# Half rows for the expert outputs of a mixture-of-experts decoder step

## The chip, the cores and the metric

The kernel runs on one core of one Trainium2 chip. The metric is the device time of one execution in microseconds (us), lower is better. Every matrix is float32.

## The reference

The reference computes one layer of a hybrid decoder for 512 prompt tokens and 8 sample tokens, D = 1024: an RMS norm, one combined projection, differential attention and indexed sparse attention in parallel, gates, an output projection and a residual. After it comes the hierarchical mixture of experts, which is all that the change touches:

```python
h = rmsnorm(x, g_ffn).reshape(b * t, d)
...
top_val, top_idx = lax.top_k(e_in_group, 2)          # inside the best of 4 groups
top_w = jax.nn.softmax(top_val, axis=-1) * g_w
...
for each of the 32 experts (wg, wu: 1024x512, wd: 512x1024):
    act = silu(h @ wg) * (h @ wu)
    out = out + (act @ wd) * combine_weight[:, None]
y = x + out
```

Each of the 520 tokens goes to two experts, so the 32 experts have 1040 token rows together, 32.5 on average. The weights of an expert are three matrices of 2 MB.

## The kernel before, in words

The kernel has four stages, each a block in which every engine has its own instruction stream: projection, attention of the prompt, merge (L1107 to L1773), and experts (L1776 on). An engine leaves a block only when all have come to its end. This document is about the last steps of merge and about the expert stage.

**Tables.** Merge routes the tokens and builds, with products of one-hot matrices on TensorE (L1342, L1347, L1351), for each expert a list of up to CAP = 64 tokens in order of rank. The list is written twice in PSUM, for partitions 0 to 63 and for 64 to 127, since the rows of tokens are handled as halves: partition p below 64 has the first 512 columns of the p-th token, partition 64 + p has the other 512. VectorE turns the list into integer tables (L1765 to L1770): `s.halves` (128 partitions) is the row number in the array of half rows, 2 x token + half, and a number beyond every bound (from NO_ROW) where the expert has no token. `s.table` (64 partitions) is the row in the prompt's output, `s.to_s` (64 partitions) the row in the sample's output, each with a number out of bounds where the row isn't there. `share(3)` and L1773 follow; the latter puts the weight of each token and expert on 128 partitions. Then merge ends.

**The loop over experts.** For expert e = 0 to 31, with two sets of buffers:
- GpSimd gathers the half rows of the expert after the next (`gather_rows`, L157): one indirect DMA, 128 rows of 2 KB from DRAM to 128 partitions; rows out of bounds are skipped.
- TensorE transposes them (L1821), VectorE copies them with the gain of the norm (L1977), TensorE multiplies by the gate and the up weights (L1827), ScalarE and VectorE make the activation (L1951, L2044, L2049), TensorE transposes it (L1833) and multiplies by the down weights (`down_product`, L1841). The result Y lies in one PSUM bank as 128 partitions of 512 columns: output columns 0 to 511 of token slot p at partition p, columns 512 to 1023 at partition 64 + p.
- ScalarE scales Y by the weights and writes y, a tile of 64 partitions of 1024 columns, in two operations (L1956), one for each half: the second reads partitions 64 to 127 and writes partitions 0 to 63. It waits for the adds of expert e - 2, which read the same buffer.
- GpSimd adds y to the outputs in DRAM (`add_rows`, L2084 to L2090): an indirect DMA with an addition to the prompt's output y_p (L2085) and one to the sample's output y_s (L2088), each over all 64 rows of 4 KB; those out of bounds write nothing.

The order on GpSimd's queue is, in pass e: wait until expert e's rows are transposed; gather for expert e + 2; wait for y of expert e - 1; wait until the adds of expert e - 2 have landed (`y_added`); issue the two adds of expert e - 1. So the adds of two experts never run beside each other, and a gather comes behind the adds that were issued before it.

**Weights.** SyncE issues the loads of the weights (L1103) in an order written out by hand, as soon as one of 4, 4 and 3 places for gate, up and down is free (`g_done`, `u_done`, `d_done`). They run in queue q1. GpSimd's DMAs run in queue q0.

**Extra blocks.** Experts with over 64 tokens get further blocks in a loop over a count that is known at run time (`extra`, `step`). VectorE prepares their tables as it does the first (L2032 to L2038). The profile of this data shows none of them carried out, but it has the tables made at the end. The last thing that SyncE waits for is `y_added`.

Of the kernel before, what the change touches and what calls it, by code (L numbers as in the profile page):

```python
# [7 lines left out]
F32, I32 = mybir.dt.float32, mybir.dt.int32  # L8
ALU = mybir.AluOpType
# [1106 lines left out]
def merge(nc, io, s):  # L1116
# [3 lines left out]
    with ExitStack() as ctx:  # L1120
# [32 lines left out]
        Lm, Lm2, C = (small[:, 40 + 32 * n:72 + 32 * n] for n in range(3))  # L1153
        unfilled, early, twice = small[:, 232:232 + NE], small[0:CAP, 264:264 + NE], small[:, 392:392 + NE]
        prank = small[:, 296:296 + 2 * NE].rearrange("p (k e) -> p k e", k=2)
# [370 lines left out]
        def _(dve):  # L1526
# [240 lines left out]
            v.tensor_tensor(s.halves[:, 0:NE], twice, unfilled, ALU.add).then_inc(table_ready, 1)  # L1767
            v.scalar_tensor_tensor(s.table[:, 0:NE], TBt[0:CAP, :], -1.0, unfilled[0:CAP, :], ALU.add, ALU.add)
            link(v.tensor_scalar(early, TBt[0:CAP, :], 1.0 + SEQ, NO_ROW, ALU.is_lt, ALU.mult))
            link(v.scalar_tensor_tensor(s.to_s[:, 0:NE], TBt[0:CAP, :], -1.0 - SEQ, early, ALU.add, ALU.add))  # L1770
            share(3)
# [4 lines left out]
def experts(nc, io, s):  # L1776


    with ExitStack() as ctx:
        sb = lambda n, sh, dt=F32: ctx.enter_context(nc.sbuf_tensor("e_" + n, sh, dt))  # L1780
        ps = lambda n, sh: ctx.enter_context(nc.psum_tensor("e_" + n, sh, F32))
        sem = lambda n: ctx.enter_context(nc.semaphore("e_" + n))
        idx = sb("idx", [128, 3], I32)
        xg = s.xg
# [4 lines left out]
        aT = sb("aT", [128, 2, 128])  # L1789
        y = [sb(f"y{n}", [CAP, D]) for n in range(2)]  # L1790
        TX, AT = ps("TX", [128, 4, 2 * CAP]), s.bankO[:, 0:256].rearrange("p (f t) -> p f t", f=2)
# [5 lines left out]
        eid = spare[:, 180:180 + NX + 1]  # L1797
        unfilled, early, twice = spare[:, 200:200 + NX], spare[0:CAP, 216:216 + NX], spare[:, 232:232 + NX]
        cmp = spare[:, 256:256 + NE * NX].rearrange("p (a b) -> p a b", a=NE)
# [144 lines left out]
        @block.scalar  # L1944
        def _(act):
            for e in range(NE):
                j = e % 2
                act.wait_ge(g_done, e + 1)
                if e:
                    act.wait_ge(a_ready, e)  # L1950
                nc.scalar.activation(sig[:], G[j][:, 0:HW], ACT.Sigmoid).then_inc(gated, 1)  # L1951
                act.wait_ge(d_done, e + 1)
                if e >= 2:
                    act.wait_ge(y_added, 32 * (e - 1))
                for h in range(2):
                    last = nc.scalar.activation(y[j][:, W * h:W * h + W], Y[j][CAP * h:CAP * h + CAP, :], ACT.Copy,  # L1956
                                                scale=s.share[CAP * h:CAP * h + CAP, e:e + 1])
                last.then_inc(y_out, 1)

            def step(act, b):  # L1960
                act.wait_ge(g_done, b + NE + 1)
                nc.scalar.activation(sig[:], G[0][:, 0:HW], ACT.Sigmoid).then_inc(gated, 1)
                act.wait_ge(d_done, b + NE + 1)
                act.wait_ge(y_added, b * 32 + NE * 32)
                for h in range(2):
                    last = nc.scalar.activation(y[0][:, W * h:W * h + W], Y[0][CAP * h:CAP * h + CAP, :], ACT.Copy,
                                                scale=s.share[CAP * h:CAP * h + CAP, bass.ds(b + NE, 1)])
                last.then_inc(y_out, 1)
                act.nop()
            extra(act, step)  # L1970

        @block.vector
        def _(dve):
# [55 lines left out]
            def tables_out():  # L2029

                dve.wait_ge(extra_tabled, 1)
                link(v.tensor_scalar(unfilled, TB[:, 0:NX], 0.0, NO_ROW, ALU.is_equal, ALU.mult))  # L2032
                link(v.tensor_scalar(twice, TB[:, 0:NX], 2.0, s.c[:, C_HALF:C_HALF + 1], ALU.mult, ALU.add))
                link(v.tensor_tensor(s.halves[:, NE:NBLK], twice, unfilled, ALU.add))
                link(v.scalar_tensor_tensor(s.table[:, NE:NBLK], TB[0:CAP, 0:NX], -1.0, unfilled[0:CAP, :], ALU.add, ALU.add))
                link(v.tensor_scalar(early, TB[0:CAP, 0:NX], 1.0 + SEQ, NO_ROW, ALU.is_lt, ALU.mult))
                link(v.scalar_tensor_tensor(s.to_s[:, NE:NBLK], TB[0:CAP, 0:NX], -1.0 - SEQ, early, ALU.add, ALU.add))
                v.tensor_copy(s.share[:, NE:NBLK], TB[:, NX:2 * NX]).then_inc(extra_ready, 1)  # L2038
# [39 lines left out]
        def _(pool):  # L2078
# [5 lines left out]
            def add_rows(n, rows, to_s):  # L2084
                nc.gpsimd.indirect_dma_start(out=io["y_p"], out_offset=bass.IndirectOffsetOnAxis(ap=rows, axis=0),  # L2085
                                             in_=y[n][:], in_offset=None, bounds_check=SEQ - 1, oob_is_err=False,
                                             compute_op=ALU.add).then_inc(y_added, 16)
                nc.gpsimd.indirect_dma_start(out=io["y_s"], out_offset=bass.IndirectOffsetOnAxis(ap=to_s, axis=0),  # L2088
                                             in_=y[n][:], in_offset=None, bounds_check=NS - 1, oob_is_err=False,
                                             compute_op=ALU.add).then_inc(y_added, 16)  # L2090

            for e in range(NE + 1):
                if e + 2 < NE:
                    pool.wait_ge(x_turned, e + 1)
                    gather_rows(nc, s, e % 2, s.halves[:, e + 2:e + 3])
                if e == NE:
                    n_extra = extra_blocks(pool)
                if e:
                    pool.wait_ge(y_out, e)
                if e >= 2:  # L2100
                    pool.wait_ge(y_added, 32 * (e - 1))
                if e:
                    add_rows((e - 1) % 2, s.table[:, e - 1:e], s.to_s[:, e - 1:e])

            def step(pool, b):
                pool.wait_ge(y_added, b * 32 + NE * 32)
                pool.wait_ge(x_turned, b + NE)
                nc.gpsimd.tensor_copy(idx[:, 0:1], s.halves[:, bass.ds(b + NE, 1)]).then_inc(idx_ready, 1)
                nc.gpsimd.tensor_copy(idx[0:CAP, 1:2], s.table[:, bass.ds(b + NE, 1)]).then_inc(idx_ready, 1)
                nc.gpsimd.tensor_copy(idx[0:CAP, 2:3], s.to_s[:, bass.ds(b + NE, 1)]).then_inc(idx_ready, 1)  # L2110
                pool.wait_ge(idx_ready, b * 4 + 3)
                pool.sem_inc(idx_ready, 1)
                gather_rows(nc, s, 0, idx[:, 0:1])
                pool.wait_ge(y_out, b + NE + 1)
                pool.sem_inc(y_passed, 1)
                add_rows(0, idx[0:CAP, 1:2], idx[0:CAP, 2:3])
                pool.wait_ge(y_added, b * 32 + NE * 32 + 32)
# [8 lines left out]
def step_kernel(nc, io):  # L2126
# [14 lines left out]
    with ExitStack() as top:  # L2141
# [48 lines left out]
        s.gffn = sb("gffn", [128, KD])  # L2190
        s.table, s.ctl = sb("table", [CAP, NBLK], I32), sb("ctl", [1, NX + 1], I32)
        s.halves = sb("halves", [128, NBLK], I32)
        s.to_s = sb("to_s", [CAP, NBLK], I32)
        s.share = sb("share", [128, NBLK])
# [41 lines left out]
```

## Time and profile before

| | us |
|---|---|
| median of 3 runs (1139.65 to 1141.88) | 1140.24 |
| the profiled execution | 1139.45 |
| its span, from the first instruction to the end | 1137.6 |
| TensorE matmul busy | 1015.8 (89%) |
| VectorE busy | 433.5 (38%) |
| GpSimd busy | 302.4 (27%) |
| ScalarE busy | 243.2 (21%) |

The mean granted TensorE clock is 0.981. The span of the profiled execution is 1.85 us shorter than its own time, which lies 0.79 us under the median. In the profile, PE is TensorE, DVE VectorE, ACT ScalarE, POOL GpSimd and SP SyncE; a name like e_y is a tile of the expert stage, x_ and k_ are tiles that live longer, and g_ those of merge. A row "A <-B 5.0" says that the engine sat idle for 5.0 us before it and that B ended that. Row counts of DMA queues are packets; the share is the time that they took, of 16 DMA engines over the window.

### The profile page before, as it was taken

Reading aid. Unit: us, or ns where it says so; the run is one execution under the profiler, and the core shown is the slowest. Engines: PE = TensorE matmul, PEld = TensorE weight load, DVE = VectorE, ACT = ScalarE, POOL = GpSimd, SP = SyncE. Lnnn points to the kernel's source line nnn. Section 1 sums busy time; section 2 is a strip of 40 time slices with the busy share of each in tenths; the row PEclk is TensorE's granted clock in tenths of the full one; section 3 lists DMA queues with packets and bytes.
Section 4 is the critical chain, followed back from the end, with each engine's and each line's share of the span. In section 5 each row is a group of like instructions: output and inputs, shape, how many; then the busy total and the mean of one; then the engine's idle time right before and its main releaser. Section 6 shows DMA issues by size and latency. Waiting matters only on the chain. (4 is left out here: it accounts for less than half of the span.)

```text
span 1137.6 us, 15848 instructions
## 1 busy us (share of the span) xinstructions
PE 1015.8 (89%) x5861; PEld 563.7 (50%) x5861; DVE 433.5 (38%) x1202; ACT 243.2 (21%) x550; POOL 302.4 (27%) x262
## 2 busy tenths in 40 slices
PE   6999999998999999998999679999987877777776
PEld 3644444445777776332455444455444434444443
DVE  3545888886566574322324411111110111011122
ACT  2122221212444545301024201111111110111011
POOL 1023513532555444001000113233322212221222
PEclk9999999999999999999999789999999999999999
DMA  6330232217656444888392789999999999999993
GB/s 207 94 109 20 75 103 103 94 44 244 195 191 212 141 135 159 315 328 296 110 426 94 277 361 412 414 421 416 412 416 419 423 416 416 416 423 415 418 411 118
DMA packets 82465, 304.26 MB, mean 267 GB/s; under 512 B 23117, under 2 KB 27341, under 8 KB 70227
## 3 DMA queue, kind: packets, MB, share of 16 engines
q1 hardware_dynamic: 64658, 273.47, 61.4%
q0 software_dynamic: 9824, 16.98, 5.1%
q10 hardware_dynamic: 7904, 12.78, 3.1%
q8 instruction: 47, 0.77, 0.3%
q14 instruction: 32, 0.25, 0.1%
HBM read 290.09 MB, written 29.72 MB: 281 GB/s over the span
## 5 line engine op out<-in xcount | busy, mean ns | idle before, releaser
L404 PE MATMUL p_z<-k_w,k_xT 128*128 128x512 f32 (+2 forms) x528 | 208.9, 550 | 0.3 <-DMA k_w<-in_w_in 0.3
L404 PEld LDWEIGHTS p_z<-k_w,k_xT 128*128 128x128 f32 (+1 forms) x528 | 92.2, 188 | 103.2 <-issue 101.4
L872 PE MATMUL a_G<-k_xT,k_w 128*128 128x260 f32 x512 | 127.2, 393 | 0.0
L2044 DVE TENSOR_TENSOR e_hid<-e_hid,e_G 128x256 f32<-128x256 f32 x32 | 13.5, 421 | 259.1 <-ACT e_hid L1951 259.1
L1956 ACT ACTIVATE e_y<-e_Y,x_share 64x512 f32<-64x512 f32 x64 | 43.7, 683 | 303.9 <-PE e_Y L1841 286.5
L872 PEld LDWEIGHTS a_G<-k_xT,k_w 128*128 128x128 f32 x512 | 92.9, 191 | 26.6 <-issue 13.8
L967 POOL TENSOR_TENSOR k_x<-k_x 128x512 f32<-128x512 f32 x64 | 80.5, 1271 | 89.5 <-DVE k_side L1033 69.2
L2085 POOL DMA_INDIRECT out_y_p<-e_y,x_table x32 | 46.2, 1443 | 201.9 <-ACT e_y L1956 132.5
L157 POOL DMA_INDIRECT k_rows<-token_rows,x_halves x32 | 33.7, 1054 | 155.4 <-PE e_TX L1821 144.7
L1243 PE MATMUL g_ring<-k_oT,k_w 128*128 128x512 f32 x128 | 60.1, 616 | 0.0
L2049 DVE TENSOR_TENSOR e_hid<-e_hid,e_U 128x256 f32<-128x256 f32 x32 | 13.5, 421 | 116.9 <-PE e_U L1827 116.9
L942 ACT ACTIVATE a_prob<-a_masked,a_nb 128x128 f32<-128x128 f32 (+3 forms) x64 | 36.0, 562 | 70.2 <-DVE a_nb L1047 70.2
L2088 POOL DMA_INDIRECT out_y_s<-e_y,x_to_s x32 | 45.4, 1420 | 9.8 <-issue 9.8
L1841 PE MATMUL e_Y<-k_xT,e_aT 128*64 128x512 f32 x176 | 40.2, 598 | 8.5 <-DVE e_aT L2053 8.5
L1841 PE MATMUL e_Y<-x_page,e_aT 128*64 128x512 f32 x176 | 40.2, 598 | 7.2 <-DVE e_aT L2053 7.2
L1033 DVE TENSOR_REDUCE k_side<-k_x 128x8 f32<-128x512 f32 x64 | 43.1, 674 | 1.5 <-POOL k_x L967 1.4
L1841 PE MATMUL e_Y<-x_w_out,e_aT 128*64 128x512 f32 x160 | 36.5, 598 | 6.6 <-DVE e_aT L2053 6.6
L556 POOL TENSOR_TENSOR p_tb<-p_t,q_rg 128x512 f32<-128x512 f32 (+1 forms) x20 | 35.4, 1772 | 22.0 <-DVE p_t L614 22.0
L1827 PE MATMUL e_G<-x_w_out,e_xT 128*64 128x256 f32 x256 | 32.2, 404 | 8.2 <-DMA x_w_out<-in_w_gate 8.2
L548 POOL TENSOR_SCALAR p_rs<-p_ms 128x8 f32<-128x8 f32 (+1 forms) x20 | 3.9, 195 | 132.5 <-DVE p_ms L581 132.5
L1827 PE MATMUL e_G<-k_w,e_xT 128*64 128x256 f32 x256 | 32.3, 405 | 7.2 <-DMA k_w<-in_w_gate 6.4
L1243 PEld LDWEIGHTS g_ring<-k_oT,k_w 128*128 128x128 f32 x128 | 23.8, 194 | 29.5 <-issue 29.2
(357 smaller groups left out, 1476.1 us busy)
## 6 DMA issues: line engine op xcount, KB each, us to landing
k_w<-in_w_in SPq DMA_DIRECT2D x11, 2048.0 KB, 8.8
k_xT<-in_w_down SPq DMA_DIRECT2D x11, 2048.0 KB
x_page<-in_w_down SPq DMA_DIRECT2D x10, 2048.0 KB, 38.5
x_w_out<-in_w_down SPq DMA_DIRECT2D x10, 2048.0 KB
k_w<-in_w_gate SPq DMA_DIRECT2D x8, 2048.0 KB, 37.1
k_w<-in_w_up SPq DMA_DIRECT2D x8, 2048.0 KB
k_oT<-in_w_gate SPq DMA_DIRECT2D x8, 2048.0 KB
k_side<-in_w_up SPq DMA_DIRECT2D x8, 2048.0 KB
```

Of the source, the lines that this page charges most:

```text
L404: last = nc.tensor.matmul(z[u % 3][0:p, 0:WIDTH[k]], s.xT[:, j, 128 * i:128 * i + p], s.w[:, c % 2, j, 0:WIDTH[k]], start=j == 0, stop=j = ...
L556: nc.gpsimd.tensor_tensor(tb[0:p, :].rearrange("p (h d) -> p h d", h=H), t0[0:p, :].rearrange("p (h d) -> p h d", h=H), bcast(s.rg[0:p, g, ...
L872: last = nc.tensor.matmul(G[u % 2][:, 0:HT], s.w[:, q % 2, j, 128 * c:128 * c + 128], s.xT[:, j, HT * h:HT * h + HT], start=j == 0, stop=j ...
L942: nc.scalar.activation(prob[:, n % 4, 0:w], masked[:, n % 3, 0:w], ACT.Exp, bias=nb[:, n:n + 1], scale=DH ** -0.5, accum_out=sums[:, n:n + ...
L967: nc.gpsimd.tensor_tensor(prods[:, m % 2, :], page[:, m % KEY_PLACES, :], qB[:, nq % 2, :], ALU.mult).then_inc(k_used, 1)
L1033: nc.vector.tensor_reduce(s.sT[k][:, n, H * b:H * b + H], prods[:, m % 2, :].rearrange("p (h d) -> p h d", h=H), AX.X, ALU.add).then_inc(k ...
L1243: last = nc.tensor.matmul(bank[:], s.wo[k][:, j, first:first + 128], x[:, j, 0:SEQ], start=j == 0, stop=j == NB - 1)
L1827: last = nc.tensor.matmul(pair(bank[CAP * h:CAP * h + CAP, 0:HW]), xT[:, j, b, :], own(weight_row(s, n, r, b), h), start=b == 0, stop=b == ...
L1841: last = nc.tensor.matmul(bank[CAP * h:CAP * h + CAP, :], aT[:, b % 2, CAP * (b // 2):CAP * (b // 2) + CAP], weight_row(s, 2, r, b)[:, W * ...
L1956: last = nc.scalar.activation(y[j][:, W * h:W * h + W], Y[j][CAP * h:CAP * h + CAP, :], ACT.Copy, scale=s.share[CAP * h:CAP * h + CAP, e:e ...
L2085: nc.gpsimd.indirect_dma_start(out=io["y_p"], out_offset=bass.IndirectOffsetOnAxis(ap=rows, axis=0), in_=y[n][:], in_offset=None, bounds_c ...
L2088: nc.gpsimd.indirect_dma_start(out=io["y_s"], out_offset=bass.IndirectOffsetOnAxis(ap=to_s, axis=0), in_=y[n][:], in_offset=None, bounds_c ...
```

## The change

The output tiles y keep the shape that Y has in PSUM, 128 partitions of 512 columns. One ScalarE operation of 128 partitions takes the place of the two of 64. The adds go over 128 rows of 2 KB with the outputs seen as arrays of half rows, and take their row numbers for the prompt from `s.halves`, the table of the gather. `s.table` and the VectorE operation that made it are gone; `s.to_s` is made on 128 partitions from `twice`. The same is done to the tables and to the loop of the extra blocks, which has two copies of indices on GpSimd instead of three.

```diff
@@ merge
-            v.scalar_tensor_tensor(s.table[:, 0:NE], TBt[0:CAP, :], -1.0, unfilled[0:CAP, :], ALU.add, ALU.add)
-            link(v.tensor_scalar(early, TBt[0:CAP, :], 1.0 + SEQ, NO_ROW, ALU.is_lt, ALU.mult))
-            link(v.scalar_tensor_tensor(s.to_s[:, 0:NE], TBt[0:CAP, :], -1.0 - SEQ, early, ALU.add, ALU.add))
+            link(v.tensor_scalar(early, TBt, 1.0 + SEQ, NO_ROW, ALU.is_lt, ALU.mult))
+            link(v.scalar_tensor_tensor(s.to_s[:, 0:NE], twice, -2.0 * SEQ, early, ALU.add, ALU.add))
@@ experts
-        y = [sb(f"y{n}", [CAP, D]) for n in range(2)]
+        y = [sb(f"y{n}", [128, W]) for n in range(2)]
+        y_half = {n: io["y_" + n].rearrange("t (h d) -> (t h) d", h=2) for n in "ps"}
...
-                for h in range(2):
-                    last = nc.scalar.activation(y[j][:, W * h:W * h + W], Y[j][CAP * h:CAP * h + CAP, :], ACT.Copy,
-                                                scale=s.share[CAP * h:CAP * h + CAP, e:e + 1])
-                last.then_inc(y_out, 1)
+                nc.scalar.activation(y[j][:], Y[j][:], ACT.Copy, scale=s.share[:, e:e + 1]).then_inc(y_out, 1)
...
             def add_rows(n, rows, to_s):
-                nc.gpsimd.indirect_dma_start(out=io["y_p"], out_offset=bass.IndirectOffsetOnAxis(ap=rows, axis=0),
-                                             in_=y[n][:], in_offset=None, bounds_check=SEQ - 1, oob_is_err=False,
+                nc.gpsimd.indirect_dma_start(out=y_half["p"], out_offset=bass.IndirectOffsetOnAxis(ap=rows, axis=0),
+                                             in_=y[n][:], in_offset=None, bounds_check=2 * SEQ - 1, oob_is_err=False,
                                              compute_op=ALU.add).then_inc(y_added, 16)
...
-                    add_rows((e - 1) % 2, s.table[:, e - 1:e], s.to_s[:, e - 1:e])
+                    add_rows((e - 1) % 2, s.halves[:, e - 1:e], s.to_s[:, e - 1:e])
...
-                nc.gpsimd.tensor_copy(idx[0:CAP, 1:2], s.table[:, bass.ds(b + NE, 1)]).then_inc(idx_ready, 1)
-                nc.gpsimd.tensor_copy(idx[0:CAP, 2:3], s.to_s[:, bass.ds(b + NE, 1)]).then_inc(idx_ready, 1)
-                pool.wait_ge(idx_ready, b * 4 + 3)
+                nc.gpsimd.tensor_copy(idx[:, 1:2], s.to_s[:, bass.ds(b + NE, 1)]).then_inc(idx_ready, 1)
+                pool.wait_ge(idx_ready, b * 3 + 2)
...
-                add_rows(0, idx[0:CAP, 1:2], idx[0:CAP, 2:3])
+                add_rows(0, idx[:, 0:1], idx[:, 1:2])
```

The second add, to y_s, is changed as the first, and so are the ScalarE operation and the tables of the extra blocks.

## Rows read from the trace of the kernel before

**Rows 1.** The page, part 2: the span in forty slices.
```profile
PE   6999999998999999998999679999987877777776
...
DMA  6330232217656444888392789999999999999993
GB/s 207 94 109 20 75 103 103 94 44 244 195 191 212 141 135 159 315 328 296 110 426 94 277 361 412 414 421 416 412 416 419 423 416 416 416 423 415 418 411 118
```

**Rows 2.** Stretches of the expert stage: length, busy per engine, PEclk, DMA share, GB/s.
```profile
665.00:668.00 3.00, 3.00 (x28) 1.78 (x26) 0.26 (x1) 0.38 (x1) 0.00 (x0) 0.94 0.06 22
675.00:813.00 138.00, 132.31 (x950) 69.38 (x948) 20.52 (x44) 19.23 (x33) 43.16 (x33) 1.00 1.01 416
813.00:1116.00 303.00, 238.56 (x1647) 128.99 (x1645) 44.08 (x102) 34.59 (x59) 72.28 (x55) 0.99 1.01 416
```

**Rows 3.** The chain that ended last, in order of time, its end.
```profile
1076.52 43.32 DMA e_up<-in_w_up
...
1129.03 0.48 ACT e_y L1956
...
1129.73 0.69 ACT e_y L1956
...
1131.20 0.41 POOL out_y_p L2085
...
1132.92 1.42 POOL out_y_s L2088
```

**Rows 4.** DVE around the end of the merge stage, from the timeline.
```profile
647.55 0.18 DVE L1768 SCALAR_TENSOR_TENSOR x_table<-x_O,g_scp 64x32 int32<-64x32 f32 x1
647.65 0.17 DVE L1769 TENSOR_SCALAR g_scp<-x_O 64x32 f32<-64x32 f32 x1
...
650.33 0.19 DVE L1773 COPY x_share<-x_O 128x32 f32<-128x32 f32 x1 [1.13 <-PE x_O L1351]
...
650.90 0.61 PE L1895 MATMUL x_O<-x_Cpre,k_c 128*128 128x32 f32 x2 [0.68 <-PEq L1120]
```

**Rows 5.** Groups by line and shape, whole span: busy, mean ns, idle before and its releaser.
```profile
L2085 POOL DMA_INDIRECT out_y_p<-e_y,x_table x32 | 46.2, 1443 | 201.9 <-ACT e_y L1956 132.5 <-DMA out_y_s<-e_y,x_to_s 69.4
L2088 POOL DMA_INDIRECT out_y_s<-e_y,x_to_s x32 | 45.4, 1420 | 9.8 <-issue 9.8
L1956 ACT ACTIVATE e_y<-e_Y,x_share 64x512 f32<-64x512 f32 x64 | 43.7, 683 | 303.9 <-PE e_Y L1841 286.5 <-DMA out_y_s<-e_y,x_to_s 17.0
...
L157 POOL DMA_INDIRECT k_rows<-token_rows,x_halves x32 | 33.7, 1054 | 155.4 <-PE e_TX L1821 144.7 <-POOLq L1120 9.7 <-issue 1.0
...
L921 ACT ACTIVATE a_prob<-a_prob,a_inv 128x512 f32<-128x512 f32 x8 | 5.7, 711 | 0.0
```

**Rows 6.** DMA packets in 1128 to 1137.6 us, the last two adds alone.
```profile
DMA packets 161, 0.19 MB, mean 19 GB/s; under 512 B 117, under 2 KB 117, under 8 KB 160
...
q0 software_dynamic: 160, 0.18, 14.9%
```

**Rows 7.** DMA packets in 1001.7 to 1002.7 us, a gather's rows arriving.
```profile
q0 software_dynamic: 23, 0.09, 22.9%
```

**Rows 8.** DMA packets in 1008 to 1012 us, an add's rows leaving.
```profile
q0 software_dynamic: 92, 0.14, 17.7%
```

**Rows 9.** DMA packets in 868 to 872 us, only empty rows and counts on q0.
```profile
q1 hardware_dynamic: 120, 1.72, 100.5%
q0 software_dynamic: 52, 0.00, 0.7%
```

**Rows 10.** GpSimd's timeline, where TensorE sets the pace.
```profile
805.87 1.44 POOL L2085 DMA_INDIRECT out_y_p<-e_y,x_table  x1 [7.41 <-DMA out_y_s<-e_y,x_to_s]
...
818.61 1.44 POOL L2085 DMA_INDIRECT out_y_p<-e_y,x_table  x1 [7.63 <-DMA out_y_s<-e_y,x_to_s]
```

**Rows 11.** GpSimd's timeline, where the weights set the pace.
```profile
1003.64 1.44 POOL L2085 DMA_INDIRECT out_y_p<-e_y,x_table  x1 [5.00 <-ACT e_y L1956]
...
1019.87 1.44 POOL L2085 DMA_INDIRECT out_y_p<-e_y,x_table  x1 [5.34 <-ACT e_y L1956]
```

More of the change, by code:

```diff
@@ L1153, in merge @@
         Lm, Lm2, C = (small[:, 40 + 32 * n:72 + 32 * n] for n in range(3))
-        unfilled, early, twice = small[:, 232:232 + NE], small[0:CAP, 264:264 + NE], small[:, 392:392 + NE]
+        unfilled, early, twice = (small[:, n:n + NE] for n in (232, 264, 392))
         prank = small[:, 296:296 + 2 * NE].rearrange("p (k e) -> p k e", k=2)
@@ L1782, in experts @@
         sem = lambda n: ctx.enter_context(nc.semaphore("e_" + n))
-        idx = sb("idx", [128, 3], I32)
+        idx = sb("idx", [128, 2], I32)
         xg = s.xg
@@ L1797, in experts @@
         eid = spare[:, 180:180 + NX + 1]
-        unfilled, early, twice = spare[:, 200:200 + NX], spare[0:CAP, 216:216 + NX], spare[:, 232:232 + NX]
+        unfilled, early, twice = (spare[:, n:n + NX] for n in (200, 216, 232))
         cmp = spare[:, 256:256 + NE * NX].rearrange("p (a b) -> p a b", a=NE)
@@ L1964, in step @@
                 act.wait_ge(y_added, b * 32 + NE * 32)
[L1965 to L1968, printed above, removed]
+                nc.scalar.activation(y[0][:], Y[0][:], ACT.Copy, scale=s.share[:, bass.ds(b + NE, 1)]).then_inc(y_out, 1)
                 act.nop()
@@ L2034, in tables_out @@
                 link(v.tensor_tensor(s.halves[:, NE:NBLK], twice, unfilled, ALU.add))
-                link(v.scalar_tensor_tensor(s.table[:, NE:NBLK], TB[0:CAP, 0:NX], -1.0, unfilled[0:CAP, :], ALU.add, ALU.add))
-                link(v.tensor_scalar(early, TB[0:CAP, 0:NX], 1.0 + SEQ, NO_ROW, ALU.is_lt, ALU.mult))
-                link(v.scalar_tensor_tensor(s.to_s[:, NE:NBLK], TB[0:CAP, 0:NX], -1.0 - SEQ, early, ALU.add, ALU.add))
+                link(v.tensor_scalar(early, TB[:, 0:NX], 1.0 + SEQ, NO_ROW, ALU.is_lt, ALU.mult))
+                link(v.scalar_tensor_tensor(s.to_s[:, NE:NBLK], twice, -2.0 * SEQ, early, ALU.add, ALU.add))
                 v.tensor_copy(s.share[:, NE:NBLK], TB[:, NX:2 * NX]).then_inc(extra_ready, 1)
@@ L2084, in add_rows @@
             def add_rows(n, rows, to_s):
-                nc.gpsimd.indirect_dma_start(out=io["y_p"], out_offset=bass.IndirectOffsetOnAxis(ap=rows, axis=0),
-                                             in_=y[n][:], in_offset=None, bounds_check=SEQ - 1, oob_is_err=False,
+                nc.gpsimd.indirect_dma_start(out=y_half["p"], out_offset=bass.IndirectOffsetOnAxis(ap=rows, axis=0),
+                                             in_=y[n][:], in_offset=None, bounds_check=2 * SEQ - 1, oob_is_err=False,
                                              compute_op=ALU.add).then_inc(y_added, 16)
-                nc.gpsimd.indirect_dma_start(out=io["y_s"], out_offset=bass.IndirectOffsetOnAxis(ap=to_s, axis=0),
-                                             in_=y[n][:], in_offset=None, bounds_check=NS - 1, oob_is_err=False,
+                nc.gpsimd.indirect_dma_start(out=y_half["s"], out_offset=bass.IndirectOffsetOnAxis(ap=to_s, axis=0),
+                                             in_=y[n][:], in_offset=None, bounds_check=2 * NS - 1, oob_is_err=False,
                                              compute_op=ALU.add).then_inc(y_added, 16)
@@ L2190, in step_kernel @@
         s.gffn = sb("gffn", [128, KD])
-        s.table, s.ctl = sb("table", [CAP, NBLK], I32), sb("ctl", [1, NX + 1], I32)
+        s.ctl = sb("ctl", [1, NX + 1], I32)
         s.halves = sb("halves", [128, NBLK], I32)
-        s.to_s = sb("to_s", [CAP, NBLK], I32)
+        s.to_s = sb("to_s", [128, NBLK], I32)
         s.share = sb("share", [128, NBLK])
```

## The prediction

> **What bounds the kernel now.** First the forty slices: from the 24th on the DMA engines stand at 9 of 10 and move 411 to 426 GB/s in nearly every slice, while TensorE falls from 9 to 7 [rows 1]. So the stage to look at is the loop over experts, and its resource is the traffic of weights. The stretches say it more sharply [rows 2]: from 675 to 813 us both are full (TensorE 132.31 of 138 us, DMA share 1.01); from 813 to 1116 us TensorE is busy for 238.56 of 303 us and the DMA share is still 1.01. One stretch is empty: from 665 to 668 us the share is 0.06, because every place for weights was full and the first expert's product had yet to free one. From there on the end of the loop is a start plus bytes over rate.
>
> The chain that ended last confirms it: the last long wait is a load of up weights, 43.32 us up to 1119.85 us; then the last expert runs without cover, ScalarE from 1129.03 us, GpSimd's two adds from 1131.20 and 1132.92 us, and the landing of the second until the span ends at 1137.6 us [rows 3]. So three things can move the time: what comes before the loop's first product, the DMA engines' work per expert, and the tail behind the last load.
>
> **ScalarE.** Removed: two operations of 64x512, 683 ns each, 64 in all, 43.7 us of busy time [rows 5]. Added: one of 128x512 for each expert. No such form from PSUM with a scale for each partition is in the trace; the nearest is L921, 128x512 at 711 ns [rows 5], so the number of partitions costs next to nothing and I take 0.69 us, between 0.68 and 0.72. For 31 experts this gives nothing: TensorE waits for weights, and GpSimd's add waits for the landing of the earlier ones where TensorE sets the pace, 7.63 us before the one at 818.61 us [rows 10]. Under the last expert all of it counts: ScalarE now works from 1129.03 to 1129.73 + 0.69 = 1130.42 us, 1.39 us; it will be 0.69. **Minus 0.70 us.**
>
> **VectorE.** L1768 goes. It is not chained to the next one, so its cost is the step between the starts, 647.55 to 647.65 us, 0.10 us [rows 4]. Is it covered? VectorE is the last to leave merge: L1773 runs at 650.33 us for 0.19, and the first TensorE work of the next block comes at 650.90 us, 0.38 us later [rows 4]. The gathers, the first product, and so the restart of the loads after the empty stretch [rows 2] follow from it. **Minus 0.10 us.** The two operations that go from 64 to 128 partitions cost nothing: L1769 on 64 took 0.17 us and L1773 on 128 0.19 us [rows 4]. At the tail the table for extra blocks is off the path. The step loop isn't run.
>
> **GpSimd.** The adds are 64 instructions of 1443 and 1420 ns; the gather, with 128 indices and rows of 2 KB as the adds will have, is 1054 ns [rows 5]. So the new price isn't in the trace. Lower bound 1.05 us each: the addition costs nothing to describe and the half rows are as the gather's. Upper bound 2.88 us: the time goes by indices, and these double. I take 1.43, no change: the gather's 128 indices cost less than 64 of an add, so the index can't carry most of the cost. Two adds lie on the tail: between minus 0.76 and plus 2.9 us, taken as **0**.
>
> **The DMA engines.** Bytes stay: a valid row of 4 KB becomes two of 2 KB. What could change is packets and what each costs. The last two adds, alone in their window, have 160 packets on q0, 0.18 MB, and 117 under 512 B [rows 6]: 128 rows and 32 counts of the 16 engines. So a row of 4 KB is one packet now, and an empty row is a tiny one. Does a half row become a packet of its own? Of a gather, whose rows are 2 KB, one us shows 23 packets with 0.09 MB, about 4 KB for each [rows 7]: two half rows travel in one packet. I take the same for the adds: 64 packets for 128 half rows, as now. The time for each byte: 17.7% of 16 engines over 4 us, 11.3 us, for 0.14 MB, some 34 rows, is about 0.32 us for a row [rows 8], for the gather 22.9% of 16 us over 23 packets, 0.16 us [rows 7]: an add moves its bytes twice, and what is charged is bytes. **0**, if they pair. If they don't, 64 more tiny or split packets for each add come to 128 for each expert. A window of them alone shows 52 packets at 0.7% of 64 us, 9 ns each, with q1 at 100.5% [rows 9]: 128 x 9 ns / 16 is 0.07 us per expert, at most 2.2 us for 31. Their turns in the queue are another matter (second rival).
>
> The Trainium skill, DMA: Bandwidth & Descriptors, section "SWDGE vs HWDGE vs iDMA", says that a packet of such a queue is preferably up to 4096 B and is the boundary at which an engine switches queues. By that rule the count of packets stays; rows 7 agree. Its section "Why small descriptors are slow" speaks against the change: each operation carries 32 B of metadata besides a fixed cost per packet. If a row of 4 KB is one operation now, that is 128 more for each expert, 4 KB of traffic or an estimated 0.01 us at 416 GB/s, 0.3 us for the whole loop. No row shows it.
>
> **The sum.** 0.70 + 0.10 = 0.80 us less. Against the profiled execution: 1139.45 - 0.80 = 1138.65. That one lies 0.79 us under the median of the runs, so against the median 1140.24 - 0.80 = **1139.4 us**. A measurement of this kernel can tell about 0.2%, 2.3 us, from no change, so this counts as the same.
>
> **Rivals.** First, the add gets the gather's price on GpSimd: 0.37 us less for each, 0.76 us with both on the tail, so 1140.24 - 0.80 - 0.76 = 1138.7. For: same index count and row size. Against: the addition has to be described. It is still within 0.2%; more would need a shorter landing too. Chance 0.14.
>
> Second, slower by much: half rows of an add don't share packets. Its place is the wait for `y_added`, in which GpSimd holds the next adds. Where TensorE sets the pace, an add goes out at 805.87 and the next at 818.61 us, behind a wait of 7.63 us for the landing of the one before [rows 10]: a cycle of 12.74 us, of which issuing takes 1.44 + 0.30 + 1.42 = 3.16 us and landing 9.6. In it each engine has (64 + 16) x 2 / 16 = 10 packets of the adds, and waits its turn behind weights; with 144 for each add it has 18. At the same wait for each turn, landing takes 9.6 x 1.8 = 17.2 us, the cycle 20.4. But slower experts ask for fewer weights, so turns get shorter: the loop now passes 138 / 12.74 + 303 / 16.23 experts (16.23 from 1003.64 to 1019.87 us [rows 11]), some 29.5 in 441 us or 14.9 us for each, and with c for the cycle, c = 3.2 + 17.2 x 14.9 / c, so c = 17.7 us. The loop then takes 29.5 x 17.7 = 522 us: plus 81, about 1220. It decides from a cycle of 14.9 us, that is from about 12 packets for each engine. For: twice as many rows, and no row shows an addition with rows of 2 KB. Against: rows 7. The Trainium skill, same page, section "Queues, rings and completion order", has the engine take turns between queues by packets, which is this mechanism. Chance 0.12.
>
> Third, GpSimd's price goes by indices, 2.88 us each: plus 2.9 us on the tail and the cycle of 12.74 up to 15.6, over the 14.9 that the loop allows. With the cycle's part hidden 1142.3; with 0.7 us on 29.5 experts 1163. Against: the gather's 1.05 us. Chance 0.10.
>
> That the change doesn't do what it says is small: one operation on 128 partitions would have to take as long as two, which L921 excludes.
>
> **How the numbers follow.** The forecast has 0.64, its own range 1138.3 to 1140.9 (the bounds of ScalarE and an uncertain tail, and what runs differ by). Faster by over 0.2% (under 1138.0) takes an eighth of it and a part of the first rival: 0.10. Slower (over 1142.5): the second rival and two thirds of the third, 0.20. The rest, 0.70, is no change. The range goes from 1137.9, below the first rival, to 1142.8, the mild end of the third; outside it are the second rival and half of the third, and little on the fast side.
>
> **What would show it.** In the changed profile: L1956's successor 32 times at 0.68 to 0.72 us; the first add after ScalarE 0.7 us closer to the last down product; both adds at 1.43 us (first rival 1.05, third 2.88); 160 packets in the tail's window (288 by the second rival), and GpSimd's cycle at some 12.7 us where TensorE sets the pace; the DMA share at 1.01 over 675 to 1116 us; the first TensorE work of the expert block 0.1 us earlier. The prediction is wrong if the adds' cycle goes above 14.9 us, or if the weights' rate of 416 GB/s changes.

## The result, and the profile after

The changed kernel takes **1159.05 us** (median of 4 runs, 1156.46 to 1162.36) beside 1141.06 us for the kernel before on the same chip: a ratio of 1.0159, 95% interval 1.0128 to 1.0189. It is slower, and it lies outside the range 1137.9 to 1142.8. The profiled execution has 1158.48 us and a span of 1156.6 us, 19.0 us more than before.

The page of the changed kernel, the slices of part 2 and queue q0 of part 3 (packets, MB, share of 16 engines):

```profile
PE   6999999998999999989999499978787796878887
...
DMA  6231132226656446797482889999999999999971
GB/s 204 94 105 34 60 110 101 83 100 216 225 154 221 118 143 234 266 368 240 193 342 111 339 354 414 418 424 413 411 413 411 395 417 410 416 420 408 418 301 20
...
q0 software_dynamic: 13920, 17.00, 5.3%
```

and q0 on the page of before:

```profile
q0 software_dynamic: 9824, 16.98, 5.1%
```

The DMA rows look as in [rows 1]; q0 doesn't: 13920 packets for the same 17.0 MB instead of 9824. The difference is 4096, that is 32 experts x 2 adds x 64: **every add has 64 packets more**. The time of q0's packets hardly grows, from 5.1 to 5.3% of the 16 engines' span. TensorE is busy to the very end, also in the last slice, in which only 20 GB/s are moved. The stretches of the changed kernel (length, PE, PEld, DVE, ACT, POOL busy, PEclk, DMA share, GB/s):

```profile
675.00:813.00 138.00, 120.26 (x848) 62.55 (x844) 17.62 (x38) 10.15 (x20) 35.55 (x26) 0.95 1.02 417
813.00:1116.00 303.00, 245.49 (x1606) 123.93 (x1608) 38.33 (x84) 18.41 (x38) 78.90 (x57) 0.90 1.01 411
1116.00:1124.00 8.00, 7.48 (x52) 3.63 (x50) 3.98 (x12) 0.29 (x1) 3.63 (x3) 1.00 0.70 239
1124.00:1150.00 26.00, 24.39 (x175) 12.65 (x171) 5.92 (x16) 2.32 (x5) 9.35 (x6) 1.00 0.15 19
```

Against [rows 2]: in the first stretch TensorE is busy for 120.26 instead of 132.31 us, so it isn't the limit there any more, while the DMA share is still 1.02. The weights run nearly as before (411 instead of 416 GB/s from 813 to 1116 us) and are through shortly after 1124 us; from 1124 to 1150 us only 19 GB/s are moved, and TensorE works off what it lags behind. That lag is what the 19 us consist of. The groups by line and shape, from the page of the changed kernel:

```profile
L2078 POOL DMA_INDIRECT out_y_p<-e_y,x_halves x32 | 50.5, 1580 | 328.8 <-ACT e_y L1955 279.0
...
L1955 ACT ACTIVATE e_y<-e_Y,x_share 128x512 f32<-128x512 f32 x32 | 22.0, 687 | 425.2 <-DMA out_y_s<-e_y,x_to_s 356.8
L1821 PE MATMUL e_TX<-k_c,k_rows 128*128 128x128 f32 x128 | 25.3, 330 | 68.7 <-DMA k_rows<-token_rows,x_halves 68.7
...
L2081 POOL DMA_INDIRECT out_y_s<-e_y,x_to_s x32 | 49.8, 1556 | 9.7 <-issue 9.7
L1841 PE MATMUL e_Y<-x_w_out,e_aT 128*64 128x512 f32 x160 | 46.1, 729 | 5.2 <-DVE e_aT L2046 5.2
...
L157 POOL DMA_INDIRECT k_rows<-token_rows,x_halves x32 | 34.4, 1075 | 39.9 <-PE e_TX L1821 21.7
```

Three engines wait for the adds: ScalarE 356.8 us for their landing, where it was 17.0 [rows 5], TensorE 68.7 us for gathers, GpSimd 328.8 us before the first add of each expert. On the chain that ended last, from 650 us on, the landing of the adds to y_s takes 66.7% of the time. One cycle on GpSimd and, below it, what the other engines do around its end (the changed kernel's timeline, start and length first):

```profile
859.36 1.58 POOL L2078 DMA_INDIRECT out_y_p<-e_y,x_halves  x1 [9.82 <-ACT e_y L1955]
861.25 1.55 POOL L2081 DMA_INDIRECT out_y_s<-e_y,x_to_s  x1 [0.30 <-issue]
863.11 1.08 POOL L157 DMA_INDIRECT k_rows<-token_rows,x_halves  x1 [0.30 <-issue]
877.28 1.58 POOL L2078 DMA_INDIRECT out_y_p<-e_y,x_halves  x1 [13.09 <-ACT e_y L1955]
```

```profile
876.53 0.69 ACT L1955 ACTIVATE e_y<-e_Y,x_share 128x512 f32<-128x512 f32 x1 [16.95 <-DMA out_y_s<-e_y,x_to_s]
877.11 0.37 ACT L1951 ACTIVATE e_hid<-e_G 128x256 f32<-128x256 f32 x1
...
879.77 1.12 PE L1821 MATMUL e_TX<-k_c,k_rows 128*128 128x128 f32 x4 [6.33 <-DMA k_rows<-token_rows,x_halves]
...
881.83 1.12 PE L1841 MATMUL e_Y<-x_w_out,e_aT 128*64 128x512 f32 x2 [0.52 <-DVE e_aT L2046]
```

The adds go out at 859.36 and again at 877.28 us, 17.9 us later; in [rows 10] it was 12.74. GpSimd's row names ScalarE as releaser, and can't be right: ScalarE ends at 877.22, 0.06 us before, while GpSimd needs 0.78 us from a release to its add, as the tail shows (1130.42 to 1131.20 us before). ScalarE started at 876.53 us behind the landing of the second add; the same landing released GpSimd. The gather issued at 863.11 us lands behind the adds and keeps TensorE waiting until 879.77 us. ScalarE's sigmoid of the next expert (L1951) sits in its queue behind the same wait. The down product that follows took 5.54 us for its 16 matmuls, and from this tile the mean of the whole loop is 729 ns. Before it was 598:

```profile
L1841 PE MATMUL e_Y<-x_w_out,e_aT 128*64 128x512 f32 x160 | 36.5, 598 | 6.6 <-DVE e_aT L2053 6.6
```

PEclk is 0.90 from 813 to 1116 us against 0.99 [rows 2]: for a part of the time the granted clock is the lower one, 1.2 GHz, and the slow product here comes right after TensorE stood still for 6.33 us.

The last two adds alone, in the tail behind the last down product, 1147 to 1156.6 us (DMA packets, then q0):

```profile
DMA packets 289, 0.19 MB, mean 20 GB/s; under 512 B 202, under 2 KB 202, under 8 KB 288
...
q0 software_dynamic: 288, 0.18, 15.7%
```

288 packets and not 160 [rows 6], with the same 0.18 MB: 128 rows x 2 + 32 counts. **A half row of an add is a packet of its own; a half row of a gather isn't** [rows 7].

The small terms. The end of the chain and of merge, both of the changed kernel:

```profile
1149.82 0.70 ACT e_y L1955
...
1151.29 0.41 POOL out_y_p L2078
...
1153.15 1.55 POOL out_y_s L2081
```

```profile
647.12 0.18 DVE L1768 TENSOR_SCALAR g_scp<-x_O 128x32 f32<-128x32 f32 x1
...
649.82 0.19 DVE L1772 COPY x_share<-x_O 128x32 f32<-128x32 f32 x1 [1.13 <-PE x_O L1351]
...
650.39 0.61 PE L1895 MATMUL x_O<-x_Cpre,k_c 128*128 128x32 f32 x2 [0.68 <-PEq L1120]
```

ScalarE's operation starts at 1149.82 us and takes 0.70 us, where two took 1.39; the add starts 0.77 us after its end, as before. From L1765 to L1772 VectorE takes 3.20 us (646.62 to 649.82) instead of 3.27, so L1768's removal gave 0.07 us. An add costs GpSimd 1580 and 1556 ns instead of 1443 and 1420.

### The profile page after: what moved, and what is told of

Same layout as the page of the kernel before. It is cut to its first block and busy times, and to the rows that moved or that the text cites. A ratio compares the mean times of both kernels' runs of the same rounds, so it can differ in the third digit from the quotient of the medians.

```text
span 1156.6 us, 15814 instructions
## 1 busy us (share of the span) xinstructions
PE 1031.8 (89%) x5861; PEld 562.7 (49%) x5861; DVE 433.4 (37%) x1200; ACT 219.2 (19%) x518; POOL 311.7 (27%) x262
## 3 DMA queue, kind: packets, MB, share of 16 engines
q0 software_dynamic: 13920, 17.00, 5.3%
## 5 line engine op out<-in xcount | busy, mean ns | idle before, releaser
L2078 POOL DMA_INDIRECT out_y_p<-e_y,x_halves x32 | 50.5, 1580 | 328.8 <-ACT e_y L1955 279.0
L1955 ACT ACTIVATE e_y<-e_Y,x_share 128x512 f32<-128x512 f32 x32 | 22.0, 687 | 425.2 <-DMA out_y_s<-e_y,x_to_s 356.8
L1821 PE MATMUL e_TX<-k_c,k_rows 128*128 128x128 f32 x128 | 25.3, 330 | 68.7 <-DMA k_rows<-token_rows,x_halves 68.7
L1821 PEld LDWEIGHTS e_TX<-k_c,k_rows 128*128 128x128 f32 x128 | 16.1, 162 | 82.6 <-DMA k_rows<-token_rows,x_halves 76.9
L1841 PE MATMUL e_Y<-x_page,e_aT 128*64 128x512 f32 x176 | 49.4, 713 | 5.7 <-DVE e_aT L2046 5.7
L2081 POOL DMA_INDIRECT out_y_s<-e_y,x_to_s x32 | 49.8, 1556 | 9.7 <-issue 9.7
L1841 PE MATMUL e_Y<-x_w_out,e_aT 128*64 128x512 f32 x160 | 46.1, 729 | 5.2 <-DVE e_aT L2046 5.2
L1841 PE MATMUL e_Y<-k_xT,e_aT 128*64 128x512 f32 x176 | 43.4, 637 | 5.7 <-DVE e_aT L2046 5.7
```

The lines of the kernel that those rows point to most:

```text
L1821: last = nc.tensor.transpose(TX[:, c, :], xg[j][:, 128 * c:128 * c + 128], s.ident[:])
L1841: last = nc.tensor.matmul(bank[CAP * h:CAP * h + CAP, :], aT[:, b % 2, CAP * (b // 2):CAP * (b // 2) + CAP], weight_row(s, 2, r, b)[:, W * ...
L2078: nc.gpsimd.indirect_dma_start(out=y_half["p"], out_offset=bass.IndirectOffsetOnAxis(ap=rows, axis=0), in_=y[n][:], in_offset=None, bounds ...
L2081: nc.gpsimd.indirect_dma_start(out=y_half["s"], out_offset=bass.IndirectOffsetOnAxis(ap=to_s, axis=0), in_=y[n][:], in_offset=None, bounds ...
```

## The experiments

The kernel before, on the same chips beside them, took 1140.2 to 1140.5 us. The ratio is to that kernel, also where the edit is made to the changed one.

| kernel | edit | us | ratio, 95% interval |
|---|---|---|---|
| a1 | changed, no sample add | 1138.72 | 0.9972 to 0.9996 |
| b1 | before, no sample add | 1138.38 | 0.9962 to 0.9997 |
| b3 | before, two empty adds more | 1163.59 | 1.0183 to 1.0242 |
| a2 | changed, weights in 8 KB packets | 1142.09 | 0.9999 to 1.0025 |
| b2 | before, one empty add more | 1144.92 | 1.0022 to 1.0048 |
| b5 | before, ScalarE's part alone | 1138.55 | 0.9969 to 0.9995 |
| a4 | changed, loads one expert later | 1151.41 | 1.0079 to 1.0141 |
| b6 | before, loads one expert later | 1140.87 | 0.9994 to 1.0023 |
| a3 | changed, two counts for the adds | 1141.01 | 0.9993 to 1.0021 |
| b4 | before, weights in 8 KB packets | 1142.41 | 1.0008 to 1.0038 |
| a7 | changed, loads two experts later | 1150.84 | 1.0079 to 1.0110 |
| b7 | before, last half scaled by VectorE | 1137.55 | 0.9965 to 0.9985 |

The theory to be tested, of turns: a DMA engine takes one packet of q0, then one of q1, and so on, so an add lands only after as many weight packets as it has packets of its own. The rival, of dear bytes: additions in rows of 2 KB cost the engines or the memory more.

**a1 and b1, the sample's add left out.** In a1, and the same on the rows of 4 KB in b1:

```diff
-                nc.gpsimd.indirect_dma_start(out=y_half["s"], out_offset=bass.IndirectOffsetOnAxis(ap=to_s, axis=0),
...
-                    pool.wait_ge(y_added, 32 * (e - 1))
+                    pool.wait_ge(y_added, 16 * (e - 1))
```

a1: 

> The kernel after, without the add to the sample's output (that part of y_s is left out). Theory of turns: an add lands only when each DMA engine has taken its packets one at a time between weight packets, so the number of packets sets the cycle. Here each engine has 9 in a cycle (18 in the changed kernel, 10 before), so the cycle falls under the 14.9 us that the weights allow and the time comes back to that of the kernel before less the second add on the tail: 1137 to 1140 us. Rival, dear bytes: adding rows of 2 KB costs the DMA engines or the memory more than rows of 4 KB. The add left out carries 16 half rows of 1040 pairs at most, so nothing but the tail would change: 1155 to 1158 us.

b1: 

> The kernel before, without the add to the sample's output. Theory of turns: 5 packets for each engine instead of 10, but the cycle of 12.7 us was already under what the weights allow, so only the tail gets shorter, by one add of 1.42 us and its gap of 0.3 us: 1138 to 1140 us. If the adds' turns already cost time in the kernel before, more: under 1136 us.

a1 took 1138.72 us, b1 1138.38. Nine packets for each engine instead of 18 and the loss is gone, though all but 16 pairs of the half rows are still added in 2 KB. The stretches of a1:

```profile
675.00:813.00 138.00, 131.97 (x948) 69.08 (x946) 20.50 (x44) 11.77 (x22) 28.96 (x22) 1.00 1.02 415
813.00:1116.00 303.00, 238.66 (x1648) 129.17 (x1646) 44.08 (x102) 21.02 (x39) 48.69 (x37) 0.99 1.01 414
```

TensorE's 131.97 and 238.66 us are those of [rows 2] within 0.4 us. By b1 the ten packets cost the kernel before no more than the tail: 2.1 us less (the interval allows 0.3 to 4.3), of which the add and its gap are 1.7.

**b3 and b2, empty adds.** To the kernel before, further adds for each expert, two in b3 and one (`range(1)`) in b2, with a table of which every row is out of bounds:

```diff
+                for _ in range(2):
+                    nc.gpsimd.indirect_dma_start(out=io["y_s"], out_offset=bass.IndirectOffsetOnAxis(ap=s.none[:, 0:1], axis=0),
+                                                 in_=y[n][:], in_offset=None, bounds_check=NS - 1, oob_is_err=False,
+                                                 compute_op=ALU.add).then_inc(y_added, 16)
```

b3: 

> The kernel before with two further adds for each expert, 64 rows each, all out of bounds, so no byte of data is added; 20 packets for each engine in a cycle instead of 10. Theory of turns: as slow as the changed kernel or slower, for GpSimd also issues two more, 3.4 us: cycle 17 to 19 us where weights are loaded, 1160 to 1195 us. Rival, dear bytes: only the tail gets longer, by 3.4 us: 1143 to 1146 us.

b2: 

> The kernel before with one further add for each expert, 64 rows, all out of bounds: 15 packets of adds for each engine in a cycle, between 10 and the 18 of the changed kernel, and no byte of data more. Theory of turns with a threshold: from 10 packets at 12.7 us and 18 at some 16.8 us, 15 make about 15.2 us, just over the 14.9 us that the weights allow, so the lag behind the weights is 0.3 us for each of 30 experts and the tail has one add more, 1.7 us: 1142 to 1150 us, much less than half of what the changed kernel lost for over half of its packets. If packets cost in proportion, without a threshold: 5 of 8 packets, 18 x 5 / 8 = 11 us, 1151 to 1154 us.

b3 took 1163.59 us: 20 packets, none of the new ones with data, and rows of 4 KB. Its groups by line and shape:

```profile
L2093 POOL DMA_INDIRECT out_y_s<-e_y,x_none x64 | 91.3, 1427 | 19.5 <-issue 19.5
...
L2086 POOL DMA_INDIRECT out_y_p<-e_y,x_table x32 | 46.7, 1458 | 236.3 <-DMA out_y_s<-e_y,x_none 231.1 <-ACT e_y L1957 5.2
```

GpSimd waits 231.1 us for the landing of adds that add nothing. The rival falls: it gave 1143 to 1146 us. But b3's further adds also take GpSimd 3.4 us of issuing in each cycle, and so b3 alone doesn't tell turns from issuing; a2, where issuing is untouched, does. b2, with 15 packets, took 1144.92 us: 4.4 us over the kernel before, of which 1.7 are the third add on the tail. Its adds' cycle has a mean of 15.3 us (28 cycles, 680.05 to 1108.15 us). So the loss isn't proportional and begins between 10 and 15 packets, as a cycle that reaches 14.9 us demands.

**a2 and b4, smaller weight packets.** Gate and up weights in two DMAs each, 8 KB for each partition:

```diff
+        halved = lambda *slots: [[(0, ap[:, 0:4]), (4, ap[:, 4:8])] for ap in slots]
-        s.ew = [whole(s.w[:, 0], ...
+        s.ew = [halved(s.w[:, 0], ...
```

a2: 

> The kernel after, with each load of gate and up weights as two DMAs of half the rows, so that a weight packet is 8 KB instead of 16 KB. Theory of turns: behind two of three weight matrices a turn takes half the time, the landing of 18 packets falls from some 14 to some 9 or 10 us, and the cycle is under the weights' 14.9 us: 1138 to 1142 us. Rival, dear bytes or a dearer description on GpSimd: no change, 1156 to 1160 us.

b4: 

> The kernel before with gate and up weights in packets of 8 KB. Its adds have slack, so their shorter turns bring nothing; the changed kernel with the same edit moved 411 GB/s instead of 416 to 418, and its weights ended 4.6 us later than those of the kernel before. So: 1143 to 1146 us, slower than the changed kernel with this edit (1142.1 us). If the rate wasn't what was left over there, but the adds: 1140 to 1141 us.

a2 took 1142.09 us, at the upper end of its forecast, so 17 of the 18 us come back with the adds untouched. The length of a turn matters, as the theory has it. DMA packets from 850 to 900 us, of a2 and then of the kernel before:

```profile
DMA packets 3630, 20.56 MB, mean 411 GB/s; under 512 B 1161, under 2 KB 1161, under 8 KB 1765
...
q1 hardware_dynamic: 2375, 19.54, 93.1%
```

```profile
DMA packets 2422, 20.94 MB, mean 419 GB/s; under 512 B 744, under 2 KB 744, under 8 KB 1192
...
q1 hardware_dynamic: 1652, 20.04, 94.2%
```

More packets move slightly less, 20.56 MB instead of 20.94. b4 took 1142.41 us, 0.6 below its forecast: the smaller packets cost the kernel before about 2 us, and a2 isn't better than b4 beyond what the runs differ by. The changed kernel has the same test inside its own trace. The up weights of every fourth expert are loaded in pieces, with packets of 4 and 8 KB. GpSimd's adds around such a load, then q1 and q0 of that stretch (912 to 922 us) and of one with full packets (880 to 892 us):

```profile
911.90 1.58 POOL L2078 DMA_INDIRECT out_y_p<-e_y,x_halves  x1 [13.22 <-ACT e_y L1955]
...
922.63 1.58 POOL L2078 DMA_INDIRECT out_y_p<-e_y,x_halves  x1 [5.91 <-ACT e_y L1955]
```

```profile
q1 hardware_dynamic: 505, 3.46, 82.9%
q0 software_dynamic: 364, 0.31, 13.1%
```

```profile
q1 hardware_dynamic: 309, 4.47, 90.2%
q0 software_dynamic: 330, 0.22, 9.1%
```

505 packets with 3.46 MB, 6.9 KB for each, against 309 with 4.47 MB, 14.5 KB; and the cycle is 10.7 us, where the one from 877.28 to 893.86 us is 16.6. The second stretch also shows the turns themselves: 330 packets of q0 beside 309 of q1, nearly one for one. How long a turn is can be worked out from [rows 9]: 100.5% of 64 us for 1.72 MB is an estimated 0.61 us for 16 KB. Of the 13.7 us from the end of the second add's issue to the landing (862.80 to 876.5 us), 18 such turns make 11.0.

**a4 and b6, loads one expert later; a7, two.** From the tenth expert on:

```diff
-                    sp.wait_ge((g_done, u_done, d_done)[n], e - DEPTH[n] + 1)
+                    sp.wait_ge((g_done, u_done, d_done)[n], e - DEPTH[n] + (2 if e > SETTLED else 1))
```

and for a7 `(3, 3, 2)[n]` in place of 2. These were to say why only 18 us are lost.

a4: 

> The changed kernel, where SyncE loads the weights of every expert after the ninth one expert later than it could, so that at most 2.7 experts of weights wait in place instead of 3.7. Theory: the loop loses about 2 us for each expert against the weights, and only what it lags at their end is paid, since the experts already in place then run at 12.5 us or less; the lead limits the lag, so with one expert less the weights themselves wait, and end later, while one expert fewer is left to catch up: 5 to 12 us above the changed kernel, 1164 to 1172 us. If the lead plays no part (the loss is a fixed one of each add): 1157 to 1161 us.

b6: 

> The same later loads in the kernel before. Its loop has no lag of its own; 2.7 experts of weights in the queues are 17 MB, 40 us at 416 GB/s, so the DMA engines don't run dry: 1140 to 1143 us. More than 1150 us would mean that the lead is needed for another reason, and that the run on the changed kernel says little.

a4 took 1151.41 us, faster than the changed kernel where I expected 5 to 12 us slower: a miss. b6 took 1140.87, as expected. a4's trace shows what happens. GpSimd's adds, then q0 and q1 from 764 to 771 us:

```profile
760.61 1.58 POOL L2078 DMA_INDIRECT out_y_p<-e_y,x_halves  x1 [12.81 <-ACT e_y L1955]
...
766.03 1.58 POOL L2078 DMA_INDIRECT out_y_p<-e_y,x_halves  x1 [0.60 <-issue]
...
771.67 1.58 POOL L2078 DMA_INDIRECT out_y_p<-e_y,x_halves  x1 [0.82 <-issue]
```

```profile
q0 software_dynamic: 519, 0.36, 32.1%
q1 hardware_dynamic: 9, 0.15, 10.3%
```

The later wait makes one pause in the weights (q1: 9 packets), and in it the cycle is 5.4 and 5.6 us instead of 17.6 (742.97 to 760.61 us). Nearly all of it is GpSimd's own issuing of two adds and a gather, 4.81 us. So a cycle is long only while weights stream. As many long cycles pass as fit in the time of the weights, and the rest of the 31 are short, in a pause or at the end. That made a forecast for a7:

> The changed kernel with the gate and up loads of the experts after the ninth issued two experts later than they could be, the down loads one later. The run with one expert less of lead contradicted the theory that the lead protects the loop: it was 8 us faster. New theory: a cycle of adds takes 16.8 us while weights stream and about 6 us while they pause; weights stream for some 447 us in every variant, which holds 26.6 slow cycles of the 31; the other 4.4 run in a pause or at the end. So it doesn't matter much where the pause lies, and this run is within 3 us of the one before it: 1148 to 1154 us. If less lead were good in itself, in proportion: 1142 to 1146 us. If the queues run dry now (1.7 experts are 25 us of loads): over 1158 us.

a7 took 1150.84 us, 0.6 from a4: where and how long the pause is doesn't matter. Why a pause in the middle is 8 us better than catching up at the end is argued, not shown by itself: in a4 TensorE has several experts in store in the pause and GpSimd alone sets the pace, at the end TensorE's own 12.5 us an expert does (the changed kernel's last add comes 12.5 us after the one before it).

**a3, two counts.** The changed kernel, where each add waits for its own kind alone:

```diff
-                                             compute_op=ALU.add).then_inc(y_added, 16)
+                                             compute_op=ALU.add).then_inc(s_added, 16)
...
-                    pool.wait_ge(y_added, 32 * (e - 1))
+                    pool.wait_ge(y_added, 16 * (e - 1))
```

with a wait for `s_added` before the sample's add alone, and for both on ScalarE.

> The changed kernel with a count of its own for the adds to the sample's output, so that the add to the prompt's output waits for the prompt's add before it alone, and is described while the packets of the sample's are still being taken. Packets stay 18 for each engine in a cycle, and 5 more of a gather. Theory of turns: 23 packets at one weight packet of 0.61 us each are 14.0 us, and what goes on top of it now, the description and the start of an add with an empty queue, is covered: cycle 14.5 to 15.5 us instead of 16.8, time 1141 to 1150 us. If the description on GpSimd or the adds' own bytes set the cycle: 1157 us or more.

It took 1141.01 us, at the lower end of its forecast. GpSimd's timeline of a3:

```profile
876.94 1.58 POOL L2081 DMA_INDIRECT out_y_p<-e_y,x_halves  x1 [4.35 <-ACT e_y L1957]
880.90 1.55 POOL L2086 DMA_INDIRECT out_y_s<-e_y,x_to_s  x1 [2.38 <-DMA out_y_s<-e_y,x_to_s]
...
893.03 1.58 POOL L2081 DMA_INDIRECT out_y_p<-e_y,x_halves  x1 [4.35 <-ACT e_y L1957]
894.91 1.55 POOL L2086 DMA_INDIRECT out_y_s<-e_y,x_to_s  x1 [0.30 <-issue]
```

The prompt's add of one expert is issued at 876.94 us while the sample's of the one before is being taken, and the sample's waits 2.38 us; the cycle, 16.1 us, is again that of the weights. All 288 packets are there. So the loss needs both: many packets (the kernel before has the same wait without the loss) and a wait that holds back both adds until both of the expert before have landed. The change isn't worth making even so: a3 can't be told from the kernel before (0.9993 to 1.0021).

**b5 and b7, the ScalarE part alone.** b5 writes one 128x512 operation into tiles of its own, and the adds take a tile of zeros:

```diff
-                for h in range(2):
-                    last = nc.scalar.activation(y[j][:, W * h:W * h + W], Y[j][CAP * h:CAP * h + CAP, :], ACT.Copy,
...
+                nc.scalar.activation(yw[j][:], Y[j][:], ACT.Copy, scale=s.share[:, e:e + 1]).then_inc(y_out, 1)
```

> The kernel before with ScalarE's one operation of 128x512 for each expert into tiles of their own, while the adds go out as before, 64 rows of 4 KB, from a tile of zeros (what the experts add to y is left out). It is the change's ScalarE part alone. By the prediction's step: minus 0.70 us on the tail and nothing in the loop, 1139 to 1140.5 us beside 1140.5 for the kernel before. If the ScalarE part had a cost of its own (the adds earlier beside the last load): 1141 us or more.

b7 leaves the tiles alone and gives the last expert's second half to VectorE:

```diff
+            dve.wait_ge(d_done, NE)
+            dve.wait_ge(y_added, 32 * (NE - 2))
+            v.tensor_scalar(y[(NE - 1) % 2][:, W:D], Y[(NE - 1) % 2][CAP:128, :], s.share[CAP:128, NE - 1:NE], None, ALU.mult).then_inc(last_half, 1)
```

> The kernel before, where for the last expert alone VectorE scales the second half of the outputs beside ScalarE's first, so the tail is short of one operation of 0.69 us while the adds keep their rows of 4 KB and their 10 packets. By the prediction's tail step: minus 0.7 us, 1139.8 us beside 1140.5 us, and within 0.2% of it. If the time moves by 2 us or more, as ScalarE's part alone did (1138.6), something besides the tail gained there.

b5 took 1138.55 us and b7 1137.55 us, which beats both kernels: 0.15 to 0.35% under the one before. The forecasts were 1139 to 1140.5 and 1139.8, so both came out lower. For b5 the interval (0.6 to 3.5 us less) still holds the 0.7 us that I gave it; for b7 (1.7 to 4.0 us less) it doesn't. The end of the chain of b7:

```profile
1128.44 0.77 DVE e_y L2066
...
1130.03 0.41 POOL out_y_p L2090
...
1131.76 1.42 POOL out_y_s L2093
```

Against [rows 3], from the last down product's end to the first add it takes 1.61 us instead of 2.19 (1128.42 to 1130.03, 1129.01 to 1131.20), 0.58 us less. The other 1.9 us of the two profiled spans (1137.6 and 1135.1) are in places that the edit doesn't touch: the last load ends 0.6 us earlier (1119.25 instead of 1119.85), and from the start of the last add to the end of the span it takes 3.3 us instead of 4.7. The second isn't the chance of one execution. Of the kernels that end with the sample's add, that stretch is 4.7 to 4.8 us in the profiles of the three with two ScalarE operations in the tail (before, b4, b6), and 3.3 to 3.8 us in the seven others (changed, a2, a3, a4, a7, b5, b7). So one ScalarE operation in place of two goes with a shorter landing of the last add, by some 1.2 us. The gain is measured; why that landing is shorter stays open.

## Why the prediction was wrong

- **What bounds the loop**: right as read for the kernel before. But the sentence that the end is "a start plus bytes over rate" holds only as long as nothing else has a longer cycle. The adds' cycle of 12.74 us was 2.2 us from that.
- **ScalarE, minus 0.70**: right, 0.69 us for the operation (687 ns on the mean) and 0.70 gone from the tail (1149.82 to 1151.29 us instead of 1129.03 to 1131.20). b5 bears out the sign.
- **VectorE, minus 0.10**: right in kind, 0.07.
- **GpSimd, 0**: 0.14 us more for each add, 0.28 on the tail. The argument that indices can't carry the cost held; the third rival fell.
- **The DMA engines, 0, "if they pair"**: this is the step that failed. "I take the same for the adds: 64 packets for 128 half rows" carried a gather's row over to an addition. An add's half rows each have a packet: 144 for each add instead of 80. Bytes were indeed free, and so, nearly, were the packets as such (q0's share 5.3% instead of 5.1%); their turns weren't, and with 18 instead of 10 in a cycle the adds' cycle went from 12.7 to 17.9 us, past the 14.9 us of the weights. The Trainium skill, DMA: Bandwidth & Descriptors, section "SWDGE vs HWDGE vs iDMA", has packets preferably of up to 4096 B. That is an upper bound, which an add's packets of 2 KB keep as well; that rows are joined up to it was read into it. Its section "Queues, rings and completion order", with the turn by packets, is what a2, b3 and the fourth-expert cycles agree with.
- **The second rival** had the mechanism, the wait and the count (288 packets) right, at a chance of 0.12; the price of 81 us was over four times too high. The term that was mis-sized is the loop's time, 29.5 experts at 17.7 us. The first 26 cycles have a mean of 16.3 us (678.37 to 1101.85 us), for every fourth is short; and the last five, as the weights run out, have 9.9 us. I let a slower loop stretch the weights; in fact they ran on into free places, at 411 to 417 GB/s and a share of 1.01 to 1.02, until they were done, and after that the adds were quick. That its 17.7 us meets the 17.9 at 877.28 us is in part luck, for it had the turns grow shorter with fewer weights.
- **What would show it** named the right views: packets in the tail's window and GpSimd's cycle. The chance was the mistake: with no row of an addition of this size, 0.12 for this case rested on a row of another kind of transfer.

## What to carry to other kernels

Count packets, not only bytes, for every small indirect DMA that runs beside a bulk stream: here each waited for a bulk packet, so what matters is packets for each engine times the length of a bulk packet (an estimated 0.61 us for 16 KB), against the period of the loop that waits for the landing. A cycle that has slack today is a threshold. Fewer packets (a1), smaller bulk packets (a2, 1142.1 us) and a split wait (a3, 1141.0 us) each brought the time back; only the split wait keeps both the sample's add and the bulk packets as they are. An empty row cost a turn like a full one (b3).

## What was not expected of the hardware

- A gather's rows of 2 KB travel in pairs, an addition's one by one, from the same queue.
- 160 packets more for each expert that carry no data cost 23 us in all (b3), of which 3.4 are the adds on the tail, while the rate from 850 to 900 us is 414 GB/s against 419: the engines look as busy as before.
- Two adds with 288 packets land at most 1.2 us after GpSimd has issued them in a4's pause in the weights, and 13.7 us after it while weights stream. The first is the cycle of 5.42 us less 3.43 us of issuing and 0.78 us to GpSimd's next add, and an upper bound, for GpSimd was still issuing a gather meanwhile; the second is 862.80 to 876.5 us in the changed kernel.
